# A decoder layer on one core: the two halves of each transposed activation, stored word by word beside each other

## The reference

```python
x = x + 0.5 * swiglu(rmsnorm(x, ffn1_norm), ffn1_w_gate, ffn1_w_up, ffn1_w_down)      # inner width 5632
h = rmsnorm(x, mix_norm)
... = jnp.split(h @ w_in, split_at, axis=-1)          # 4096 columns for HGRN2, 1840 for sparse attention
o_hg = hgrn2_mix(...)                                 # 8 heads, gated linear recurrence
o_nsa = nsa_mix(...)                                  # 16 query heads, compressed, selected and window branch
x = x + jnp.concatenate([o_hg, o_nsa], axis=-1) @ w_out
x = x + mem_cross_attn(rmsnorm(x, xattn_norm), rmsnorm(mem, mem_norm), wq, wk, wv, wo)   # 4 heads, 256 memory tokens
x = x + 0.5 * swiglu(rmsnorm(x, ffn2_norm), ffn2_w_gate, ffn2_w_up, ffn2_w_down)
return rmsnorm(x, final_norm)
```

## Time and profile before

| | |
|---|---|
| median of 3 runs | 2152.39 us (2148.71 to 2154.0) |
| the profiled execution, its own time | 2151.12 us |
| its span, first to last instruction | 2149.2 us |
| mean granted clock of PE over the span | 0.977 |
| PE matmul busy | 97%, 9679 matmuls |
| PE weight load busy | 80%, 9679 loads |
| DVE, ACT busy | 52%, 44% |
| DMA | 372 MB, 173 GB/s on average |

### The profile page before, as it was taken

One profiled execution on the slowest core, in us unless ns is written; L12 is line 12 of the kernel. 1 busy time (PEld: TensorE's weight loads), 2 busy tenths in 40 slices (PEclk: granted clock), 3 DMA queues, 4 the chain that ended last, 5 costly groups with the idle time before them and its releaser, 6 DMA issues.

```text
span 2149.2 us, 25561 instructions
## 1 busy us (share of the span) xinstructions
PE 2088.2 (97%) x9679; PEld 1728.5 (80%) x9679; DVE 1117.6 (52%) x1400; ACT 940.5 (44%) x1181; POOL 0.2 (0%) x4
## 2 busy tenths in 40 slices
PE   6999999999999999999999999899999999999997
PEld 5788888888888888878888987678888888888886
DVE  5545454454544445676567555454544545444444
ACT  6544444444444445454453244444444444433442
POOL 0000000000000000000000000000000000000000
PEclk9999999999999999999997699899999999999999
DMA  6566666666565655665540055266666666755553
GB/s 224 176 196 186 193 187 187 190 190 188 186 191 179 191 186 176 195 219 158 152 147 1 18 184 178 72 175 189 186 191 188 191 190 185 209 187 189 187 189 124
DMA packets 194343, 372.23 MB, mean 173 GB/s; under 512 B 12904, under 2 KB 15456, under 8 KB 194144
## 3 DMA queue, kind: packets, MB, share of 16 engines
q1 hardware_dynamic: 190176, 366.62, 56.5%
q10 hardware_dynamic: 4096, 4.64, 0.6%
HBM read 369.11 MB, written 2.10 MB: 173 GB/s over the span
## 4 chain that ended last, share of the span: by engine, by line
PE 94%; DVE 2%; ACT 2%; ACTq 1%; issue 1%; DVEq 0%
PE psum L1202 87%; PE psum L1213 2%; PE psum L1484 1%; PE psum L1438 1%; PE psum L1306 1%; PE psum L1406 0%; PE psum L1419 0%; ACT w_hi L422 0%; DVE xT_lo L780 0%; ACT xT_hi L445 0%; ACT silu_gate L452 0%; PE psum L1570 0%; DVE att L1089 0%; DVE w_lo L744 0%; ACTq L475 0%
## 5 line engine op out<-in xcount | busy, mean ns | idle before, releaser
L744 DVE TENSOR_TENSOR w_lo<-w_raw,w_hi 128x1024 fp32r<-128x1024 f32 x696 | 850.5, 1225 | 920.3 <-ACT w_hi L422 919.1
L422 ACT ACTIVATE w_hi<-w_raw 128x1024 fp32r<-128x1024 f32 x696 | 736.5, 1060 | 1041.5 <-PE psum L1202 1028.9
L1202 PE MATMUL psum<-w_hi,xT_hi 128*128 128x512 f32 (+1 forms) x1824 | 712.6, 391 | 7.7 <-DVE xT_lo L780 4.9
L1202 PE MATMUL psum<-w_hi,xT_lo 128*128 128x512 f32 (+1 forms) x1824 | 708.0, 388 | 0.0
L1202 PE MATMUL psum<-w_lo,xT_hi 128*128 128x512 f32 (+1 forms) x1824 | 707.9, 388 | 0.0
L1202 PEld LDWEIGHTS psum<-w_hi,xT_hi 128*128 128x128 f32 x1824 | 342.8, 188 | 80.1 <-DVE xT_lo L780 6.2
L1202 PEld LDWEIGHTS psum<-w_hi,xT_lo 128*128 128x128 f32 x1824 | 342.8, 188 | 70.4
L1202 PEld LDWEIGHTS psum<-w_lo,xT_hi 128*128 128x128 f32 x1824 | 342.9, 188 | 68.6
L1202 PE MATMUL psum<-w_hi,ffT_hi 128*128 128x512 f32 x928 | 369.4, 398 | 2.4 <-DVE ffT_lo L1169 2.4
L1202 PE MATMUL psum<-w_hi,ffT_lo 128*128 128x512 f32 x928 | 367.3, 396 | 0.0
L1202 PE MATMUL psum<-w_lo,ffT_hi 128*128 128x512 f32 x928 | 367.1, 396 | 0.0
(11 more groups left out here) (199 smaller groups left out, 709.0 us busy)
## 6 DMA issues: line engine op xcount, KB each, us to landing
w_raw<-in_g SPq DMA_DIRECT2D x176, 512.0 KB, 3.6
w_raw<-in_u SPq DMA_DIRECT2D x176, 512.0 KB, 3.7
w_raw<-in_d SPq DMA_DIRECT2D x176, 512.0 KB, 4.2
w_raw<-in_w_in SPq DMA_DIRECT2D x88, 512.0 KB, 3.6
w_raw<-in_w_out SPq DMA_DIRECT2D x32, 512.0 KB, 3.6
w_raw<-in_wk SPq DMA_DIRECT2D x8, 512.0 KB, 4.7
w_raw<-in_wv SPq DMA_DIRECT2D x8, 512.0 KB, 4.0
w_raw<-in_cw SPq DMA_DIRECT2D x8, 512.0 KB, 3.8
```

The costliest lines, as they stand in the source:

```text
L422: nc.scalar.activation(w_hi[:, slot], w_raw[:, slot], ACT.Copy).then_inc(w_hi_ready, 1)
L744: nc.vector.tensor_tensor(w_lo[:, slot], w_raw[:, slot], w_hi[:, slot].bitcast(F32), ALU.subtract)\
L1202: mm = nc.tensor.matmul(dst[:, t, 0:width], act_t, w[:, slot, kk, 0:width], start=(first and kk == 0 and n == 0), stop=(last and kk == KT_ ...
```

## The change

The hi and the lo part of a block become one tensor of pairs: word 2i is hi of token i, word 2i + 1 is lo. `xT_hi`, `xT_lo`, `ffT_hi` and `ffT_lo` are from then on views of `xT` and `ffT` with a step of two words; all code that reads or writes them stays as it is. A stationary tile of 128 tokens is thus read with a step of two words from 1024 bytes, and ACT and DVE write, and DVE reads, with the same step. A constant `PAD` could lengthen each block's row; it is 0. The area before ffT is rounded to a multiple of 256 instead of 512, so that ffT begins at 135936 (256 more than a multiple of 512) instead of 136192; xT stays at 32896, and `w_raw`, `w_hi`, `w_lo` stay where they are. The mix tiles lie at block 24 on for both parts.

No engine's sequence of instructions changes: the same instructions stand in the same order with the same waits, only with other addresses and steps.

```diff
+PAD = 0
...
-        xT_hi = put("xT_hi", [P, KD, SEQ], F32R)
-        xT_lo = put("xT_lo", [P, KD, SEQ], F32R)
+        xT = put("xT", [P, KD, SEQ + PAD, 2], F32R)
+        xT_hi, xT_lo = (xT[:, :, 0:SEQ, i] for i in range(2))
...
-        at[0] = (at[0] + 511) // 512 * 512
+        at[0] = (at[0] + 255) // 256 * 256
         ff = at[0]
-        ffT_hi = put("ffT_hi", [P, KF, SEQ], F32R)
-        ffT_lo = put("ffT_lo", [P, KF, SEQ], F32R)
+        ffT = put("ffT", [P, KF, SEQ + PAD, 2], F32R)
+        ffT_hi, ffT_lo = (ffT[:, :, 0:SEQ, i] for i in range(2))
...
-        MIX_HI, MIX_LO, OX = 0, 6, 40
+        MIX_HI, MIX_LO, OX = 24, 24, 40
```

## The result

| | before | after |
|---|---|---|
| median of 4 runs each (before: the three of above and one more) | 2151.66 us (2148.71 to 2154.0) | 2182.2 us (2181.92 to 2182.41) |
| ratio after / before | | 1.0143, 95% 1.0125 to 1.016 |
| the profiled execution: own time, span | 2151.12, 2149.2 us | 2181.92, 2180.0 us |
| mean granted clock of PE | 0.977 | 0.981 |

The change makes the kernel slower by 30.5 us. The forecast was 2137, with a sum of -15.6 us; the time lies inside the range, on the other side of no change, and it is the number of rival C. A spacing is the time from the start of one matmul to the start of the next.

What follows compares the result with a forecast made beforehand. PE, busy 97% of the span, bounds the kernel through unit's matmuls. ffT's -15.6 us, with load, writers and mix tiles at 0, took 2152.4 to 2136.8, say 2137; range 2049 to 2205, about 0.8.

Steps and rivals of the forecast that it cites:

- rival C: xT matmuls: at equal pace a load starting in the stream's place stays there; +30 us (2182) to +98 (2250), chance 0.25.
- Rival A: ffT matmuls: nothing moves, the 5.6 ns come from the 128-byte offset or from no meeting; 2152 us, chance 0.22.
- First, the load: Stationary tile loads in unit: reading with a step of two keeps 110 ns, factor 1.0, so no cost.
- the +7 of the bound: 304-column matmuls: if the stepped load took factor 1.9, 209 ns against 138 on 96 of them, +6.8 us.
- Rival D: Stationary loads become the bound beyond factor 2.06; at 2.5 +390 us, about 2540, chance 0.08.
- The 66-column loads: 48 matmuls with 66 stationary columns at 229.6 ns, taken as evidence that xT's remaining 13.5 ns ignore load length.
- Second, the meeting: Load beside stream: the step keeps their distance, ffT falls to 226.8 ns, -15.6 us; xT keeps 226.8.
- The picture of two readers: Matmuls of unit: the stream gains 512 bytes per tile on the load, passing it mid-tile over ffT, costing 5.6 ns.
- Third, the writers: ACT and DVE stepped writes and reads of hi and lo: taken as 0, at most +15 us at stage ends.
- Fourth: Mix tiles move from 0 and 6 to 24 behind the same waits: 0.
- the uneven starts: Sign of the slower-xT case: 192 matmuls over xT in 44.6 us or more, with unevenly spaced starts.
- Rival B: All surcharge above the stream is the two reads meeting: ffT -46 us (2107), xT -58 more (2049), chance 0.17.

Runs made afterwards that it cites:

- the first two experiments: Before with the ffT area moved to the weights' place within 512 bytes: 2136.68 us; before with xT moved 128 bytes ahead of that place: 2181.02 us.
- The finer map: Microbenchmarks outside the layer, cells of 96 equal matmuls by tile step and byte distance from the moving row: float32r 226.7 ns (step 1 at 0), step 2 230.0 to 235.6.
- the kernel with whole rows: After with hi and lo of a block as whole 256-word rows side by side, same areas and mix tiles, step 1: 2151.79 us, 0.9999 of before.
- the bfloat16 cells: Microbenchmark loops of 96 matmuls with bfloat16 instead of float32r operands, 512 columns: 215.8 ns at distances 0 and 128 with steps 1 and 2.

## Why the prediction was wrong

**The ground held.** That `unit`'s matmuls set the time, that a spacing is to be read from the chain and not from the busy time, that the address is what separates ffT from xT, and the 5.6 ns for it: the first two experiments gave 226.7 and 232.4 where they were predicted, and 14.7 and 29.6 us for the 15.6 and 30.1 of the sum. Rival A, that nothing moves, gave two reasons. That the 5.6 ns come from no meeting at all does not fit, since they move with the distance; that they come with ffT's start being 128 bytes off is borne out, and ffT kept nearly all of them (231.4). What A lacks is the loss on xT.

**First, the load: right.** A factor of 1.0 was taken, and 194 / 188 is 1.03. The 304-column group went from 138 to 140 ns, 96 x 2 = 0.2 us instead of the +7 of the bound. Rival D is out: no run shows a load longer by its factor of 2.06 or 2.5. At step 3 and 4 the load grows to 253 and 309 ns, by 1.35 and 1.64, and the spacing only to 233 to 240. The 66-column loads were a poor witness for the claim that a shorter load does not help: their tiles lie 264 bytes apart, so their distances vary, and their spacing depends on what ran before.

**Second, the meeting: this step failed.** It said that with a step of two words, load and stream keep their distance, so that ffT falls to 226.8 and xT keeps 226.8. Both are wrong. With the stepped load every distance that was tried takes 230.0 to 235.6 ns, in phase too; ffT got 231.4, xT 233.3. The equal pace itself did not fail, as far as the loads' durations tell: from 64 to 128 columns the load grows by 188 - 134 = 54 ns at step 1 and by 193 - 136 = 57 at step 2, an estimated 0.84 and 0.89 ns per word. With a step of two that is 0.44 ns for each 4 bytes, nearly the stream's 0.42. What failed is that two reads at one pace and a fixed distance leave each other alone. The picture of two readers of which one overtakes the other had been drawn from two values, 226.8 and 232.4, and was carried to a case, equal pace, for which the trace has no row. The finer map shows the picture itself to be poor: the period is 256 bytes, not the 512 on which the overtaking was reckoned, and 64 columns in phase, whose load is over sooner, are dearer than 128 (230.0 against 226.7). The term of the sum that was mis-sized is 5376 x 0, which measured 5376 x 6.6, and 2784 x -5.6, which measured 2784 x -1.0.

**Third, the writers: right in the sum.** DVE's factor is 1.00 for 256 words, ACT's 1.08 for 1024 words and 1.03 for 256; the kernel with pairs in ffT only, which has all 24 long writes, is 2.5 us above the sum of its matmuls, within its interval, and the one with pairs in xT only 1.9 below; no writer is seen in the time. **Fourth**, the mix tiles: 0, as taken; the kernel with whole rows has them and is at 2151.79.

**Rival C had the place and the number, half of the reason.** It put the loss on xT, at 5376 x 5.6 = +30 us, because a load at equal pace would stay in the stream's place. That a stepped load disturbs the stream over xT is shown. That it does so because it stays in one place is not: out of place, at 128, the matmul still takes 231.4 ns, 4.7 above the 226.7 of a contiguous tile in phase; and the uneven starts that C named as its sign did not come. Its price was borrowed from ffT's 5.6 and met 6.6; that ffT came out 1.0 ns better, not untouched, and 2 us that the sum has too much, brought the total to its 2182. That its number was met is luck. **Rival B**, that the whole surcharge goes away, is out for float32r: no cell of 512 columns is below 226.7. That 216 ns can be reached is right, as the earlier trace rows and the bfloat16 cells show, but by another kind of operand, not by another meeting.

The chance of 0.25 for C against 0.28 for the forecast was honest about the missing row; the number put forward was not well guarded. The forecast needed two things of a stepped load that nothing showed, that equal pace separates and that equal pace in phase is harmless, and the second carried twice the matmuls of the first.

**What stays open** is what the two reads share. Some common spacings stand in simple ratios (226.7, 230.0 and 233.3 ns are 17, 17.25 and 17.5 times 13.33 ns, an estimate of the time of 32 columns at 2.4 GHz), which would fit two reads that are served in groups and lock to each other; that is argued, no run isolates it, and the direction of the load was not settled.

## What to carry to other kernels

Where a float32r product streams at full width, put stationary tiles at the same place as the moving rows beside them and read them with step 1. Within 512 bytes the layer shows it: one rounding line did that here for 0.9934 of the time. That the same place within 256 is enough is shown by the map alone. Nearly the same place is not enough: 4 bytes past it took 232.4 ns. A step of two words cost 6.6 ns on each 512-column matmul that had been in phase, and nothing on ffT's, which had been out of phase. With bfloat16 or float32 operands neither mattered in the cells that were tried. And before a forecast rests on how two readers behave at a pace that the trace does not have, measure that pace with a loop of equal matmuls: 96 of them show a nanosecond, if the loop is repeated after different work, since one cell alone can be 2 or 3 ns off.

## What was not expected of the hardware

- The distance of stationary tile and moving row changes a 512-column float32r matmul from 226.7 to up to 234.3 ns at step 1, with a period of 256 bytes, and a distance of 4 bytes already gives 232.4.
- Fewer stationary columns are not cheaper in phase: 128, 64, 32 at distance 0 take 226.7, 230.0, 231.7 ns, although their loads last 188, 134, 109.
- The same loop over the same addresses can settle at one of two spacings (230.0 and 233.3, 233.3 and 235.6, 232.4 and 233.4), picked by what ran just before, and keep it for 192 matmuls.
- At 256 and 384 moving columns, step 2 at distance 0 costs nothing (120.0 and 173.3 ns at either step): with 448 columns it is 0.6 ns (202.7 to 203.3), with 512 it is 6.6. At 256 columns and step 1, distance 128 is even the cheaper one (118.7 against 120.0).
